# Eight FFN weight products with their converted weights stored in woven column order and read back in order

## The reference

```python
def swiglu(h, w_in, w_out):
    g, u = split_cols(h @ w_in, (D_FF, D_FF))
    return (jax.nn.silu(g) * u) @ w_out
```

## Time and profile before

| | |
|---|---|
| median of 2 runs | 2081.52 us |
| the profiled execution: its own time | 2080.47 us |
| its span on the core | 2078.3 us |
| TensorE busy | 2056.5 us, 9627 matmuls |
| VectorE busy | 1234.5 us |
| ScalarE busy | 1113.1 us |
| DMA, mean over the span | 173 GB/s |
| granted TensorE clock | 1.0 |

### The profile page before, as it was taken

How to read it: one execution, slowest core, us unless ns; L and a number is a source line. 1 busy time by engine, 2 the same in 40 slices (tenths; PEclk the granted TensorE clock), 3 DMA queues, 4 the chain that set the end, 5 groups by cost and what they waited for, 6 DMA issues and landing times.

```text
span 2078.3 us, 25155 instructions
## 1 busy us (share of the span) xinstructions
PE 2056.5 (99%) x9627; PEld 1683.9 (81%) x9627; DVE 1234.5 (59%) x1721; ACT 1113.1 (54%) x1682; POOL 36.3 (2%) x60
## 2 busy tenths in 40 slices
PE   8999999999999999999999999999999999999999
PEld 6877888888778888888887888888888888788887
DVE  6576665565657555655557765655555466655553
ACT  5565544445665544654456665544444465665442
POOL 0000100000000000000000000000000000000000
PEclk9999999999999999999999999999999999999999
DMA  7545566555545665566564344665666563545553
GB/s 249 156 139 167 177 186 185 186 170 170 148 157 179 203 189 191 183 189 187 187 164 141 123 156 145 185 183 188 185 185 187 188 192 127 176 136 163 184 188 131
DMA packets 258215, 359.76 MB, mean 173 GB/s; under 512 B 16909, under 2 KB 152289, under 8 KB 258097
## 3 DMA queue, kind: packets, MB, share of 16 engines
q1 hardware_dynamic: 256016, 352.75, 54.5%
q0 software_dynamic: 2080, 5.41, 0.8%
HBM read 357.04 MB, written 1.06 MB: 172 GB/s over the span
## 4 chain that ended last, share of the span: by engine, by line
PE 95%; DVE 2%; ACT 1%; issue 1%; POOL 0%; DMA 0%; SPq 0%; DVEq 0%; ACTq 0%
PE M L780 29%; PE M L782 28%; PE M L781 28%; PE AUX L822 3%; PE AUX L836 1%; DVE WL L1270 1%; PE AUX L1022 1%; PE AUX L1000 1%; PE AUX L947 1%; ACT WH L1049 1%; PE AUX L962 0%; PE AUX L874 0%; DMA RAW<-in_w_in 0%; PE AUX L953 0%; DVE RET L1453 0%
## 5 line engine op out<-in xcount | busy, mean ns | idle before, releaser
L1270 DVE TENSOR_TENSOR WL<-RAW,WH 128x1024 fp32r<-128x1024 f32 x669 | 815.9, 1222 | 660.7 <-ACT WH L1049 657.9
L1049 ACT ACTIVATE WH<-RAW 128x1024 fp32r<-128x1024 f32 x669 | 706.3, 1058 | 670.5 <-PE M L782 664.1
L780 PE MATMUL M<-WH,Bh 128*128 128x512 f32 x1792 | 719.9, 402 | 3.9 <-DVE WL L1270 3.9
L782 PE MATMUL M<-WH,Bl 128*128 128x512 f32 x1792 | 700.4, 391 | 0.0
L781 PE MATMUL M<-WL,Bh 128*128 128x512 f32 x1792 | 699.5, 390 | 0.0
L780 PEld LDWEIGHTS M<-WH,Bh 128*128 128x128 f32 x1792 | 337.2, 188 | 73.5 <-DVE WL L1270 4.9
L782 PEld LDWEIGHTS M<-WH,Bl 128*128 128x128 f32 x1792 | 336.7, 188 | 72.6
L781 PEld LDWEIGHTS M<-WL,Bh 128*128 128x128 f32 x1792 | 337.7, 188 | 63.4
L1078 ACT ACTIVATE AS<-M,KEEP 128x256 f32<-128x256 f32 x132 | 55.3, 470 | 101.0 <-PE M L782 97.6
L780 PE MATMUL M<-WH,MTh 128*128 128x512 f32 x128 | 55.1, 430 | 0.0
L782 PE MATMUL M<-WH,MTl 128*128 128x512 f32 x128 | 50.5, 395 | 0.0
(11 more groups left out here) (405 smaller groups left out, 2515.4 us busy)
## 6 DMA issues: line engine op xcount, KB each, us to landing
RAW<-in_ffn_w_in SPq DMA_DIRECT2D x352, 256.0 KB, 3.2
RAW<-in_w_in SPq DMA_DIRECT2D x104, 512.0 KB, 3.8
RAW<-in_w_gate_up SPq DMA_DIRECT2D x176, 256.0 KB, 3.3
RAW<-in_ffn_w_out SPq DMA_DIRECT2D x88, 512.0 KB, 3.6
RAW<-in_w_down SPq DMA_DIRECT2D x44, 512.0 KB, 3.7
RAW<-in_x_w_kv SPq DMA_DIRECT2D x32, 512.0 KB, 3.6
RAW<-in_even_w_in SPq DMA_DIRECT2D x24, 512.0 KB, 3.9
RAW<-in_odd_w_in SPq DMA_DIRECT2D x24, 512.0 KB, 3.9
```

The source lines that it names most:

```text
L780: e.matmul(out, s.hi, wh, start=s.at0, stop=False)
L782: i = e.matmul(out, s.lo, wh, start=False, stop=s.final)
L1049: e.activation(p.WH[:, h, 0:s.size], p.RAW[:, i, 0:s.size], ACT.Copy).then_inc(k.w_hi, 1)
L1270: e.tensor_tensor(p.WL[:, h, 0:s.size], p.RAW[:, s.u % NRAW, 0:s.size], hi.bitcast(F32), ALU.subtract).then_inc(k.w_lo, 1)
```

## The change

For eight of the products, and for those only, WH and WL hold the 512 columns of a k-block in another order. Each block of 512 places is two halves of 256. The columns go by turns in groups of e: the first e columns to the first half, the next e to the second half, the next e to the first half behind the first group, and so on. ScalarE and VectorE read RAW in its own order and write (VectorE also reads WH) in jumps between the halves. TensorE's moving operand reads WH and WL by the same pattern, so that the columns arrive in their old order and the result is the same. The size e is another one in each product: 1 in gu1, 2 in f1a0, 4 in f2a0, 8 in f1b0, 16 in f1a1, 32 in f2b0, 64 in f2a1, 128 in f1b1. Since the pattern needs a dimension for each of group, half and place, a unit is converted by two instructions of 512 columns in place of one of 1024, on ScalarE and on VectorE; only the second signals. The stationary operands, the PSUM outputs, the DMAs and the semaphores' counts are untouched.

```diff
+GROUP = {"gu1": 1, "f1a0": 2, "f2a0": 4, "f1b0": 8, "f1a1": 16, "f2b0": 32, "f2a1": 64, "f1b1": 128}
+
+def woven(x, name):
+    g = GROUP.get(name)
+    return x if g is None else x.rearrange("p (h i e) -> p i h e", h=2, e=g)
+
+def plain(x, name):
+    g = GROUP.get(name)
+    return x if g is None else x.rearrange("p (i h e) -> p i h e", h=2, e=g)
...
-            wh = p.WH[:, h, s.kk * s.ncol:(s.kk + 1) * s.ncol]
-            wl = p.WL[:, h, s.kk * s.ncol:(s.kk + 1) * s.ncol]
+            name = p.unit_names[s.u]
+            wh = woven(p.WH[:, h, s.kk * s.ncol:(s.kk + 1) * s.ncol], name)
+            wl = woven(p.WL[:, h, s.kk * s.ncol:(s.kk + 1) * s.ncol], name)
             e.matmul(out, s.hi, wh, start=s.at0, stop=False)
             e.matmul(out, s.hi, wl, start=False, stop=False)
             i = e.matmul(out, s.lo, wh, start=False, stop=s.final)
...
-            e.activation(p.WH[:, h, 0:s.size], p.RAW[:, i, 0:s.size], ACT.Copy).then_inc(k.w_hi, 1)
+            name = p.unit_names[s.u]
+            if name in GROUP:
+                for c0 in range(0, s.size, 512):
+                    q = e.activation(woven(p.WH[:, h, c0:c0 + 512], name), plain(p.RAW[:, i, c0:c0 + 512], name), ACT.Copy)
+                q.then_inc(k.w_hi, 1)
+            else:
+                e.activation(p.WH[:, h, 0:s.size], p.RAW[:, i, 0:s.size], ACT.Copy).then_inc(k.w_hi, 1)
...
+            if name in GROUP:
+                for c0 in range(0, s.size, 512):
+                    q = e.tensor_tensor(woven(p.WL[:, h, c0:c0 + 512], name), plain(p.RAW[:, i, c0:c0 + 512], name),
+                                        woven(p.WH[:, h, c0:c0 + 512].bitcast(F32), name), ALU.subtract)
+                q.then_inc(k.w_lo, 1)
```

More of the change, by code:

```diff
@@ L1269, in vector @@
             e.wait_ge(k.w_hi, s.u + 1)
-            e.tensor_tensor(p.WL[:, h, 0:s.size], p.RAW[:, s.u % NRAW, 0:s.size], hi.bitcast(F32), ALU.subtract).then_inc(k.w_lo, 1)
+            name, i = p.unit_names[s.u], s.u % NRAW
+            if name in GROUP:
[3 more added lines that the diff above has]
+                q.then_inc(k.w_lo, 1)
+            else:
+                e.tensor_tensor(p.WL[:, h, 0:s.size], p.RAW[:, i, 0:s.size], hi.bitcast(F32), ALU.subtract).then_inc(k.w_lo, 1)
         elif s.kind == "rope":
```

## The result

The changed kernel takes 2161.77 us (median of 2 runs, 2161.73 to 2161.80) against 2081.52: ratio 1.0391, 95% interval 1.0375 to 1.0408. It is 80 us slower. The forecast was 113 us slower, with all of it in gu1. The sign and the wide range (2076 to 2320 us) hold; the place does not, and the time lies under the forecast's own range of 2173 to 2205 us.

The account below looks back on a forecast made before the run. TensorE's matmul pace was taken as the bound. The profiled 2080.5 us plus 113 for gu1's moving read, all else nothing, gave 2193.3, with the median 1 us above: 2194 us; own range 2173 to 2205, wide range 2076 to 2320.

Parts of the forecast that it names:

- The bound: Whole kernel: TensorE, 95% of the chain; only what changes the pace of the matmuls, 0.2267 us each, changes the time.
- Two conversions for one: Eight products, 286 units: 0.205 us more per unit on ScalarE, 0.152 on VectorE, hidden beside the matmuls, costed at nothing.
- Groups of 1 on ScalarE and VectorE: Conversions in gu1: not shown in the trace; bounds from nothing to 2.45 to 3.67 us per unit.
- VectorE becomes the bound in gu1: Rival in gu1: jumping conversions make TensorE wait for WL; 2091 us at double cost, 2141 at three times; chance 0.05.
- harsher form: VectorE rival in gu1 at three times the column cost: 16.7 us a chunk, +59 us, 2141 us; chance 0.03.
- Groups of 8 free on VectorE: VectorE conversions: groups of 8 and more free or within 11 ns, from 64-column instructions in the trace.
- The moving read, the term that counts: TensorE's moving operand: single columns in gu1 at 0.440 us a matmul, +113 us; e = 2 and above nothing.
- The reason given for 0.2267: Matmul pace: 0.0134 us over 512 columns at 2.4 GHz; its vanishing on 3432 matmuls, -46 us, 2036 us, chance 0.02.
- The rule of the Trainium skill: SBUF reads: two hits per 16-byte line needed for full bandwidth; against e = 1, clears e = 2, gives no size.
- Each jump costs: Rival over gu1, f1a0, f2a0: a clock period, 0.417 ns, per jump whatever the group; +215 us, 2297 us, chance 0.07.
- A piece of four columns: Rival: SBUF hands out four columns; e = 1 costs four times (+359 us), e = 2 double (+120); 2561 us, chance 0.15.
- The total: Whole kernel: 2194 us, 5.4% slower, with only gu1's +113 us in the sum; chance 0.37.

Follow-up runs that it names:

- all_sorted: Kernel before, every 512-column matmul reading single columns of two runs of 256 in turn, conversions reading every second RAW column and writing in order: 2029.2 us, ratio 0.9747.
- write_only: Changed kernel's conversions (woven, two instructions per unit), but matmul operands read contiguously as in the kernel before: 2084.8 us, ratio 1.0022 to the kernel before.

## Why the prediction was right, and where it was wrong

- **The bound.** Right. In every run in which the other two engines are no more than 62% busy, the paces of the matmuls account for the time to within 7 us; at 70% (all_sorted) they no longer do.
- **Two conversions for one: nothing.** Right to 4 us (write_only, 2084.8). Durations of 0.63 and 0.69 us are as read from the earlier trace rows.
- **Groups of 1 on ScalarE and VectorE.** Between the bounds: 2.25 to 2.3 us a unit on either. The rival that VectorE becomes the bound in gu1 was near; with 87% of it busy TensorE idled 1.5 us in 100, and gu1 lost about 4 us to the conversions. (Its harsher form has a slip: 3.67 + 0.15 us a unit makes 15.3 us a chunk, not 15.0, and 2145 us, not 2141.)
- **Groups of 8 free on VectorE.** Right (0.688 us per 512 columns), and 2 and 4 as well (0.690 and 0.686).
- **The moving read, the term that counts.** This step failed. It said +113 us for e = 1 and nothing for e = 2 and above; measured are -6 and +86. The step took one stream and asked how many neighbouring columns it needs per piece, so that single columns had to be the dearest order. The runs show them to be the quickest when they come from two runs by turns (0.2159 us), and pairs, which the step cleared, to be slow (0.3415). What fits these and the further orders is a model of two interleaved streams, each with that need. A doubling does occur, at 0.43 to 0.49 us, near the 0.440 priced, but in other orders: those in which a lane changes its 16 bytes at each read and doesn't return at once. That ScalarE's rate sets it is not shown.
- **The reason given for 0.2267.** The prediction saw the 0.0134 us over 512 columns at 2.4 GHz and gave 0.02 to their vanishing, because the rows show "the same pace whatever the buffers". But all buffers were read contiguously, so sameness was no evidence on the order. Single columns of two runs take 0.011 of the 0.013 away.
- **The rule of the Trainium skill** (page "SBUF — State Buffer", the note on cachelines under "Door 1: The DMA port swizzle"), at least two hits per 16-byte line, was weighed for the stream as a whole and so cleared pairs and condemned single columns. For TensorE the measurements are the reverse of that reading (0.3415 and 0.2159 us). Applied to each lane it gives the right side, quick or slow, in every order of the table where a lane's hits come in a row, if the 0.25 and 0.27 us of groups of 4 count as quick. In the conversions of the change, where ScalarE writes and VectorE writes and reads WH in jumps, it agrees as it stands: pairs 0.66 and 0.69 us, single columns 1.15 and 1.13. It does not hold for their reads of every second column, with two hits, which cost 0.48 and 0.26 us per 1024.
- **The rivals.** "Each jump costs" came nearest in f1a0 (56 us by its price, 60 measured) but put 113 us into gu1, and its flat price is refuted: per jump, e = 2 costs 0.114 / 256 = 0.45 ns, e = 4 0.18, e = 16 0.39, e = 64 nothing, and e = 1, with the most jumps, gains. "A piece of four columns" fell by gu1 as well.
- **The total.** That 2162 lies in the wide range and on the right side is luck: a loss of 113 us in the wrong place stood for one of 86 in others. The test that the prediction itself named, that a change in stretches with e of 4 or more would make it wrong as a whole, did strike: they lost 25 us of the 80.

## What to carry to other kernels

Where TensorE is the bound with float32r operands, as here, the order in which the moving operand is read is worth trying: single columns of two runs in turn ran 5% quicker than contiguous ones, while most steps and pairs took 1.5 to 2 times as long. Put the order back where it cost nothing here, in the reading of PSUM, not in the conversions. When a term of a prediction has no row, price its pieces with a small experiment of many patterns in one kernel; a total that fits proves none of them.

## What the runs showed of the hardware that was not expected

- A moving read of 512 float32r columns takes 0.2158 us with single columns of two runs at least 4 columns apart, 0.2269 to 0.2275 when contiguous, 0.43 to 0.49 when, by the model, every lane changes its 16 bytes each time and doesn't return to the last but one. The lanes are a model that orders these numbers, not something a trace shows.
- Two lines by turns in one lane lie between: 0.27 to 0.28 us with four reads on each, 0.33 to 0.34 with two. How much a lane keeps was not settled.
- Breaks between longer groups cost more than the model says, and not in proportion to their number: 0.2500, 0.2433, 0.2400, 0.2367 us for groups of 4, 8, 16, 32, then nothing at 64. In a contiguous run of which every second group is taken they go the other way: 0.2312, 0.2325, 0.2400 for 4, 8, 16. Both stay open.
- ScalarE and VectorE read every second column of PSUM in the time of contiguous ones (470 and 686 ns), but not of SBUF (1.54 and 1.48 us per 1024 against 1.06 and 1.22).
